# Expert 0's all-token columns cut from 512 to 256, its rows picked by one-hot products, and one weight piece split in halves

## What is computed

```python
def moe_swiglu(h, w_router, w_gate, w_up, w_down):
    t = h.reshape(B * S, Dm)
    logits = (t @ w_router).astype(jnp.float32)
    top_vals, top_idx = lax.top_k(logits, TOP_K)
    top_w = jax.nn.softmax(top_vals, axis=-1)
    gates = jnp.sum(jax.nn.one_hot(top_idx, N_EXPERTS) * top_w[..., None], axis=1)
    for e in range(N_EXPERTS):
        ye = swiglu(t, w_gate[e], w_up[e], w_down[e])
        out = out + gates[:, e:e + 1] * ye
```

## Time and profile before

| | |
|---|---|
| median of three runs | 1045.84 us (1043.88 to 1045.89) |
| the profiled execution | 1044.83 us, of which 1043.1 us from the first to the last instruction (the span) |
| PE busy | 1022.6 us, 98% |
| DVE, ACT, POOL busy | 270.5, 250.6, 54.4 us |
| mean granted clock of PE | 0.995 of full speed |
| weights and other data moved by DMA | 347.24 MB |

### The profile page before, as it was taken

The page is one execution under the profiler, slowest core; times in us unless marked ns, Lnnn a source line. Parts: engine busy times, 40 slices in busy tenths (PEclk is TensorE's granted clock), DMA queues, the critical chain, the costliest instruction groups (busy, mean ns, idle before and its releaser), DMA issues.

```text
span 1043.1 us, 22297 instructions
## 1 busy us (share of the span) xinstructions
PE 1022.6 (98%) x9903; PEld 579.3 (56%) x9903; DVE 270.5 (26%) x418; ACT 250.6 (24%) x426; POOL 54.4 (5%) x159
## 2 busy tenths in 40 slices
PE   8999999999999899999999999999999999999995
PEld 8987888888998654433334444444444444444331
DVE  7677545455677420000000000000000000000022
ACT  7666525345685200000000000000000000000121
POOL 4000000000101000001000001001000100100110
PEclk9999999999999999999999999999999999999998
DMA  8477656552638899999999999999999999999994
GB/s 286 180 253 273 194 179 202 183 178 80 201 113 311 290 357 361 417 419 408 419 409 417 419 418 408 417 420 408 417 418 420 399 419 419 394 393 419 417 417 164
DMA packets 125149, 347.24 MB, mean 333 GB/s; under 512 B 7368, under 2 KB 40176, under 8 KB 125056
## 3 DMA queue, kind: packets, MB, share of 16 engines
q1 hardware_dynamic: 119760, 331.64, 82.0%
q0 software_dynamic: 4560, 13.41, 3.7%
q10 hardware_dynamic: 736, 0.80, 0.2%
HBM read 341.10 MB, written 4.72 MB: 332 GB/s over the span
## 4 chain that ended last, share of the span: by engine, by line
PE 91%; DMA 4%; DVE 2%; issue 1%; ACT 1%; SPq 0%; DVEq 0%; ACTq 0%; POOLq 0%
PE ps L2011 29%; PE ps L2064 14%; PE ps L2015 10%; PE ps L1543 8%; PE ps L1545 8%; PE ps L1544 8%; PE ps L2069 5%; DMA raw_gu<-in_w_in 2%; DMA ring<-in_moe_w_down 2%; PE ps L2026 1%; DMA gains<-tok_rows,tok_row 1%; PE ps L2099 1%; PE ps L1550 0%; PE ps L1932 0%; PE ps L1717 0%
## 5 line engine op out<-in xcount | busy, mean ns | idle before, releaser
L2011 PE MATMUL ps<-ring,xg 128*32 128x512 f32 (+1 forms) x3072 | 379.6, 551 | 0.0
L2064 PE MATMUL ps<-ring,moe_ht 128*32 128x512 f32 x1408 | 177.3, 593 | 1.9 <-DMA ring<-in_moe_w_down 1.9
L2015 PE MATMUL ps<-ring,xg 128*32 128x256 f32 x2048 | 176.4, 379 | 0.0
L2011 PEld LDWEIGHTS ps<-ring,xg 128*32 128x32 f32 x3072 | 111.2, 110 | 95.7 <-issue 50.1
L2015 PEld LDWEIGHTS ps<-ring,xg 128*32 128x32 f32 x2048 | 73.2, 110 | 147.2 <-issue 147.2
L1543 PE MATMUL ps<-hi_gu,xt_hi 128*128 128x512 f32 (+1 forms) x352 | 132.1, 375 | 1.3 <-DVE lo_gu L2203 0.7
L1545 PE MATMUL ps<-hi_gu,xt_lo 128*128 128x512 f32 (+1 forms) x352 | 129.1, 367 | 0.0
L1544 PE MATMUL ps<-lo_gu,xt_hi 128*128 128x512 f32 (+1 forms) x352 | 128.8, 366 | 0.0
L1438 ACT ACTIVATE moe_silu<-ps 128x512 f32<-128x512 f32 (+1 forms) x24 | 13.3, 553 | 334.4 <-PE ps L2015 278.7
L2701 DVE COPY moe_ht<-ps 128x256 f32<-128x256 f32 (+1 forms) x18 | 7.1, 395 | 295.6 <-PE ps L2037 295.6
L2069 PE MATMUL ps<-ring,moe_ht 128*32 128x256 f32 x1056 | 81.1, 379 | 0.0
(11 more groups left out here) (326 smaller groups left out, 880.3 us busy)
## 6 DMA issues: line engine op xcount, KB each, us to landing
ring<-in_moe_w_down SPq DMA_DIRECT2D x88, 1024.0 KB, 16.7
ring<-in_moe_w_gate SPq DMA_DIRECT2D x56, 1024.0 KB, 17.5
ring<-in_moe_w_up SPq DMA_DIRECT2D x56, 1024.0 KB, 17.8
ring<-in_moe_w_gate SPq DMA_DIRECT2D x40, 768.0 KB, 16.4
ring<-in_moe_w_up SPq DMA_DIRECT2D x40, 768.0 KB, 14.3
...
raw_d<-in_dense_w_down SPq DMA_DIRECT2D x11, 1024.0 KB, 4.9
```

Of the source, the lines that this page charges most:

```text
L2011: last = pe.matmul(ps[tile(q), (B_GATE, B_UP)[part], 0:w // 2], xg[:, rows_at, k, tile(g)], weights[:, h * w // 2:(h + 1) * w // 2], start ...
L2015: last = pe.matmul(ps[tile(q), (B_GATE_B, B_UP_B)[part], 0:FC], xg[:, rows_at, k, A_SLOTS:SLOTS], weights[:, q * FC:(q + 1) * FC], start=k ...
L2064: last = pe.matmul(ps[tile(q), B_YA, :], moe_ht[:, at:at + 32], weights[:, h * 512:(h + 1) * 512], start=start, stop=stop)
```

## The change

- The all-token columns of expert 0 become 256 gate and 256 up columns. `FIRST_PIECES` is 2: a first piece now holds four steps k of 512 columns (gate and up side by side, one bank per tile), and `all_piece(j, t)` has 4 x 3 = 12 matmuls of 512 columns.
- Expert 0's remaining 2560 columns are chunks of 1024, 1024 and 512. A 512-column chunk has four k in a piece (two pieces for gate, two for up), and its B slots take 128 columns each in four strips. The first `down` has one piece instead of two; `pick_hidden` has 4 matmuls instead of 8.
- The order on PE is: piece 0 of tile 0, `route(0)`, half of piece 1, `turn_rows` of tile 1, the other half, `route(1)`, piece 0 of tile 1, `find_places`, piece 1 of tile 1, `pick_rows`. VectorE makes the low part of piece 1 in two halves, one before tile 1's post norm and one between it and tile 1's pre norm; ScalarE and VectorE no longer split pieces 2 and 3.
- `pick_rows` makes `xg` of expert 0 by 16 products of `rows` with expert 0's one-hot rows. The DMA gather, its transposes and VectorE's copy of expert 0's token numbers are gone. `xg` lies no longer over `rows` but over `gains[2]` and `pool_w_sb`.
- The ring's slots come in another order: pieces 4 and 5 wait for the splits of the mixing part, 6 to 9 for the output products, 10 and 11 for the splits of the two first pieces, 12 to 15 for `first_used`.

The core of the diff:

```diff
-B_LOGITS, B_PLACES, B_COUNTS, B_ALL, B_XG0 = 4, 4, 7, ((0, 1), (5, 6)), (3, 7)
+B_LOGITS, B_PLACES, B_COUNTS, B_ALL, B_XG0 = 4, 4, 7, (0, 5), (3, 7)
...
-    FIRST_PIECES = 4
+    FIRST_PIECES = 2
...
-    RING_ORDER = [4, 5, 14, 15] + [first_slot(j) for j in range(FIRST_PIECES)] + \
+    EARLY_SLOTS = [first_slot(j) for j in range(FIRST_PIECES, 4)]
+    RING_ORDER = [4, 5, 14, 15] + EARLY_SLOTS + [base + n for n in EARLY_SLOTS for base in (6, 10)] + \
+        [first_slot(j) for j in range(FIRST_PIECES)] + \
         [base + first_slot(j) for j in range(FIRST_PIECES) for base in (6, 10)]
 
     def width(p, c):
 
         if c < 0:
-            return WIDE
-        return 3 * FC if p == 0 or c == CHUNKS - 1 else 4 * FC
+            return FC
+        if c < CHUNKS - 1:
+            return 4 * FC
+        return 3 * FC if p else 2 * FC
 
     def col0(p, c):
 
         if c < 0:
             return 0
-        return WIDE + c * 3 * FC if p == 0 else c * 4 * FC
+        return c * 4 * FC + (0 if p else FC)
+
+    def b_width(p, c):
...
+    def k_tiles(p, c):
+
+        return 2 if width(p, c) > 2 * FC else 4
+
+    def gate_pieces(p, c):
+        return KT // k_tiles(p, c)
...
-                to = flat_piece(raw_gu, slot).rearrange("p (k w c) -> p k w c", k=2, w=2)
+                to = flat_piece(raw_gu, slot).rearrange("p (k w c) -> p k w c", k=4, w=2)
                 for part, w in enumerate((moe_w_gate, moe_w_up)):
-                    sp.dma_start(to[:, :, part, :], w[0, 0][2 * j * P:(2 * j + 2) * P, 0:WIDE]
+                    sp.dma_start(to[:, :, part, :], w[0, 0][4 * j * P:(4 * j + 4) * P, 0:FC]
                                  .rearrange("(k p) n -> p k n", p=P)).then_inc(gu_loaded[slot // 2][slot % 2], 16)
 
             def first_use(n):
@@ -811,10 +826,14 @@
                     sp.wait_ge(d_lo_done, 2 * NCH)
                 elif n < 4:
                     sp.wait_ge(attn_mm, TT * DEPTH)
-                elif n < 8:
-                    sp.wait_ge(gu_lo_done, PIECE0 + n - 4 + 1)
+                elif n < 6:
+                    sp.wait_ge(gu_lo_done, PIECE0)
+                elif n < 10:
+                    sp.wait_ge(out_mm, TT * DEPTH)
+                elif n < 12:
+                    sp.wait_ge(gu_lo_done, PIECE0 + n - 10 + 1)
                 else:
-                    sp.wait_ge(first_used, (n - 8) // 2 + 1)
+                    sp.wait_ge(first_used, (n - 12) // 2 + 1)
...
-                    w, c0 = width(p, c), col0(p, c)
-                    sp.dma_start(ring[:, slot, 0:2 * w].rearrange("p (k n) -> p k n", k=2),
-                                 expert_rows((moe_w_gate, moe_w_up)[part], e)[i * FC:(i + 1) * FC, c0:c0 + w]
+                    w, c0, kn = width(p, c), col0(p, c), k_tiles(p, c)
+                    sp.dma_start(ring[:, slot, 0:kn * w].rearrange("p (k n) -> p k n", k=kn),
+                                 expert_rows((moe_w_gate, moe_w_up)[part], e)[i * kn * P:(i + 1) * kn * P, c0:c0 + w]
                                  .rearrange("(k p) n -> p k n", p=P)).then_inc(ring_loaded[slot], 16)
...
-            gather_picked(0)
-            pool.wait_ge(tok_row_ready, 2)
-            pool.wait_ge(picked_turned, 2)
             gather_picked(1)
...
-                split_first(l, 2)
                 pre_ffn(l, 1)
-                split_first(l, 3)
...
-            def find_rows(n, some):
-                pe.wait_ge(onehots_ready, n + 1)
-                for e in some:
+            def find_rows():
+                pe.wait_ge(onehots_ready, 2)
+                for e in range(1, E):
...
-            def all_piece(j, t, between=None):
+            def all_piece(j, t, steps=(0, 1, 2, 3)):
 
                 hi, lo = flat_piece(hi_gu, first_slot(j)), flat_piece(lo_gu, first_slot(j))
                 a = slice(t * P, (t + 1) * P)
-                for k in range(2):
-                    kt = 2 * j + k
-                    if (j, t, k) == (2, 0, 0):
-                        pe.wait_ge(first_k_lo, 1)
-                    elif t == 0:
+                if t == 0:
+                    if j == 1 and steps[0] == 0:
+                        pe.wait_ge(half_piece_lo, 1)
+                    else:
                         pe.wait_ge(gu_lo_done, PIECE0 + j + 1)
-                    if k and between:
-                        between()
-                    for part in range(2):
-                        at = slice((2 * k + part) * WIDE, (2 * k + part + 1) * WIDE)
-                        last = mm3(ps[:, B_ALL[t][part], :], xt_hi[:, kt, a], xt_lo[:, kt, a], hi[:, at], lo[:, at],
-                                   kt == 0, kt == KT - 1)
+                for k in steps:
+                    kt, at = 4 * j + k, slice(k * WIDE, (k + 1) * WIDE)
+                    last = mm3(ps[:, B_ALL[t], :], xt_hi[:, kt, a], xt_lo[:, kt, a], hi[:, at], lo[:, at], kt == 0, kt == KT - 1)
                 if t == 1:
                     last.then_inc(first_used, 1)
-                elif j == 3:
+                elif j == FIRST_PIECES - 1 and steps[-1] == 3:
                     last.then_inc(all_tile0, 1)
 
             def first_chunk():
                 all_piece(0, 0)
-                all_piece(1, 0)
                 pe.wait_ge(router_lo_done, 1)
                 route(0)
-                all_piece(2, 0)
+                all_piece(1, 0, (0, 1))
                 turn_rows(1, T_FFN, 1)
-                all_piece(3, 0)
+                all_piece(1, 0, (2, 3))
                 xt_ready(1, T_FFN, 1)
                 route(1)
                 all_piece(0, 1)
                 find_places()
-                all_piece(1, 1, lambda: find_rows(0, range(1)))
-                all_piece(2, 1)
-                all_piece(3, 1, turn_first)
-
-            def turn_first():
-                pe.wait_ge(counted, 1)
+                all_piece(1, 1)
                 for part in range(2):
-                    turn_picked(0, part)
+                    pick_rows(part)
+
+            def pick_rows(part):
+                pe.wait_ge(*((counted, 1) if part else (onehots_ready, 1)))
+                for k in range(4):
+                    at = slice((part * 4 + k) * P, (part * 4 + k + 1) * P)
+                    for t in range(TT):
+                        last = pe.matmul(ps[:, B_XG0[part], k * SLOTS:(k + 1) * SLOTS], rows[:, t, at],
+                                         onehots[:, t, 0, 0:SLOTS].bitcast(F32), start=t == 0, stop=t == TT - 1)
+                last.then_inc(picked_turned, 1)
 
...
-                for k in range(4):
+                for k in range(2):
...
-                    pe.wait_ge(*((all_silu, 1) if part == GATE else (all_hidden, 1)))
+                    pe.wait_ge(all_hidden, 1 if part == GATE else TT)
                 else:
                     pe.wait_ge(silu_ready if part == GATE else hidden_ready, n)
+                kn = k_tiles(p, c)
                 for k in range(KT):
-                    slot = piece_ring(p, c, part, k // 2)
-                    if k % 2 == 0:
-                        pe.wait_ge(ring_loaded[slot], piece_level(p, c, part, k // 2, step))
-                    weights = ring[:, slot, (k % 2) * w:(k % 2 + 1) * w]
+                    slot = piece_ring(p, c, part, k // kn)
+                    if k % kn == 0:
+                        pe.wait_ge(ring_loaded[slot], piece_level(p, c, part, k // kn, step))
+                    weights = ring[:, slot, (k % kn) * w:(k % kn + 1) * w]
                     for q in range(4):
                         h, g = divmod(q, 2)
                         last = pe.matmul(ps[tile(q), (B_GATE, B_UP)[part], 0:w // 2], xg[:, rows_at, k, tile(g)],
                                          weights[:, h * w // 2:(h + 1) * w // 2], start=k == 0, stop=k == KT - 1)
                     if has_b(p):
-                        for q in range(w // FC):
-                            last = pe.matmul(ps[tile(q), (B_GATE_B, B_UP_B)[part], 0:FC], xg[:, rows_at, k, A_SLOTS:SLOTS],
-                                             weights[:, q * FC:(q + 1) * FC], start=k == 0, stop=k == KT - 1)
-                    if k % 2:
+                        wb = b_width(p, c)
+                        for q in range(b_groups(p, c)):
+                            last = pe.matmul(ps[tile(q), (B_GATE_B, B_UP_B)[part], 0:wb], xg[:, rows_at, k, A_SLOTS:SLOTS],
+                                             weights[:, q * wb:(q + 1) * wb], start=k == 0, stop=k == KT - 1)
+                    if k % kn == kn - 1:
                         last.then_inc(ring_used, 1)
...
-                split_first(l, 1)
+                split_half_piece(1, 0)
                 post_norm(l, POST_MIX, 1, banks(B_OUT[1], 2))
-                split_first(l, 2)
+                split_half_piece(1, 1)
                 pre_norm(l, PRE_FFN, 1)
-                split_first(l, 3)
                 low_part(l, T_FFN, 1)
...
-                dve.wait_ge(tok_row_mm, 1)
```

(7 more changed lines are left out.)

82 lines of the change are left out of this document (38 added, 44 removed).

## The result

The changed kernel takes **1032.8 us** (median of four runs, 1030.6 to 1033.4) against 1045.9 for the kernel before beside it (1043.9 to 1049.5): ratio 0.987, 95% interval 0.984 to 0.990, so 13 us faster. The forecast was 1034.6, a gain of 11.2. Run twice more beside the experiments, the changed kernel gave 1031.2 and 1031.6, both at a ratio of 0.987. The profiled execution took 1030.6 (span 1028.2, mean granted clock 0.996).

A forecast was written before the change was run, and what follows sets the result against it. It took TensorE's path as the bound, the weight stream close behind. Terms of -9.9, -0.9 and -0.4 sum to -11.2 us, from 1044.83 to 1033.6 profiled, median 1034.6; 80% range 1031.5 to 1038.5.

The forecast's parts named there:

- Part 1: Tile 1's norm chain up to route(1): fewer first-piece products and half splits gain 3.0 us, with 2.6 us new PE idle.
- both covers: Piece 1's half splits on VectorE hide behind ScalarE's root and square; uncovered, each would cost 1.2 us.
- Part 2: From route(1)'s start to expert 0's first gate product: 19.2 us becomes 12.35, a gain of 6.9.
- Part 3: PE's clock, at half from 363.1 to 366.5 us: without long waits, 0.9 us behind the first gate product comes back.
- I take no fall: The new PE waits of 1.6, 1.0 and 0.7 us were taken as too short to halve the clock.
- Part 4: Expert 0's chunks of 1024, 1024 and 512 columns instead of 768: 0.4 us gained in all.
- Part 5: Weight stream: earlier loads of larger pieces move it 12 to 13 us forward, PE 11.2, so PE's gain holds.
- the full ring in p = 6: At expert p = 6 the full ring restores the stream's relation to PE, so the last down-weight waits stay some 2 us.
- Rival (a): The stream was the real bound at the end: the last four waits, 1.9 us, go, giving 1032.7 us; chance 0.12.
- Nothing in this part adds or takes time: On the weight stream: its earlier start and reordered loads were priced at zero in the sum.
- Rival (c): Early loads stay held in SyncE's queue, so p = 1 waits: gain only 4 to 6 us, 1040.8; chance 0.08.
- the 1.7 us around the span: Execution time outside the profiled span, 1044.83 us against 1043.1, kept unchanged in the forecast.

The follow-up runs named there:

- whole: Changed kernel with the low part of first piece 1 split whole ahead of tile 1's last norm, instead of in halves: 1034.8 us, ratio 0.990.
- gather: Changed kernel with the old look-up, copy, indirect load and transposes for expert 0's columns put back instead of the one-hot products: 1039.6 us, ratio 0.995.
- before_pick: Kernel before with only expert 0's columns made by 16 one-hot products instead of the DMA gather: 1041.3 us, ratio 0.996.
- late4: Changed kernel with only ring pieces 8 to 11 held back until tile 1's product of the first piece is done: 1033.8 us (two runs).

## Why the prediction was right, and where not

- **Part 1**: turn_rows(1), named at 339.0, began at 337.67, and route(1), named at 342.5, at 341.12; with the 1.3 us of the start added back, 338.96 and 342.41. Waits 1.43 and 0.97 for 1.6 and 1.0. Gain 3.07 for 3.0; both covers stood as said, and *whole*, with the whole split ahead of the post norm, shows a price of 0.8 us.
- **Part 2**: pick 3.71 for 3.9, copy wait 0.57 for 0.66, distance 12.24 for 12.35. The first gate product, named at 354.8, began at 353.36, or 354.65 with the 1.3 us. Both experiments on it came out near their numbers; only gather's clock fall was three times the length I gave it.
- **Part 3**: "I take no fall" failed as a statement on the kernel: it held in the profiled execution and not in two repetitions, where PE lost 1.6 us. Its bound, 3.4 us at half, is what they show. Whether the short waits bring that fall is **open**: with the waits as they are five of nine profiles show one at 339 to 348 us, with them filled none of two, but over all runs 6 of 13 of the changed kernel and 5 of 10 of the filled ones have a mean granted clock of 0.995 or less. That mean does not tell where a fall was. The six at or under 0.995 average 1033.0 us and the other seven 1031.0.
- **Part 4**: the sign held (0.7 us gained, 0.4 forecast), two terms of it were off and nearly cancel, and one addition was wrong. I took 0.27 us for eight B records of 128 columns; they take 0.22:

```profile
412.64 0.61 PE L2025 MATMUL ps<-ring,xg 128*32 128x256 f32 x8
413.08 0.40 PE L2030 MATMUL ps<-ring,xg 128*32 128x128 f32 x8
413.30 0.61 PE L2025 MATMUL ps<-ring,xg 128*32 128x256 f32 x8
```

  A step of the short chunk is 0.65 to 0.66 us (starts 412.64 and 413.30), and the two short chunks' gate and up are 10.7 us, not 11.2. The nearest row was the wrong guide; streaming (0.21), which I had as the lower end, was right. The four of 1024 columns took 10.45 each from start to the next line's start, not 10.35: 0.4 more. And four times 10.35 and 11.2 are 52.6, not the 52.8 that I wrote; by my own terms the loss was 0.2 there, and measured it is 0.1. By the Trainium skill (TensorE: Matmul & The Clock Gate, section "Wait — 56ns, not 53.3ns?") starts are at least about 25 ns apart; the 27 ns a record here agree with it, lying just above.
- **Part 5 and the end**: the last step of the mechanism failed, and it is the largest miss. The size was right: the stream moved forward by 12 to 13 us, I wrote, and PE by 11.2. The fourth last piece now comes 14.4 us earlier, 13.1 without the start, and PE 11.6. But I went on: "the full ring in p = 6 brings both to the same relation as now", so the waits stay. They did not: 0.9 us instead of 1.9 in this profile, 0.3 and none in the repetitions, whose clock fall kept PE back. By the rows the relation is not made in p = 6. There a piece of the kernel before takes 12.3 us from issue to landing, twice the 6.3 us of gate pieces in 380:395; by that the stream had not caught up with the free slots as it had in p = 0, though its rate dips there too (370 GB/s in 905:930), for a reason that stays open. It is made in p = 0, where the new order of loads holds the stream at the slots until about 440 us instead of 410, and it was kept from there: in 910:920 it is 9.9 us to landing, a shorter queue. For a change of PE's path alone my sentence holds: before_pick and gather moved PE by 4.0 and 8.9 us and the fourth piece by 3.5 and 8.7. Whether the larger pieces of p = 0 or the earlier releases make the difference is not shown by a run of its own; late4, with the larger pieces but late releases, ends like the old order (waits 2.4 us), which points to the releases. Rival (a) gave such a gain 0.12 and priced it at 1.9; it came to 1.5 us at the waits in this profile.
- "Nothing in this part adds or takes time" was too strong. With pieces 4 to 11 held back to 346 us the whole gain is lost (1044.0), with 8 to 11 held back about 2 us of it. Rival (c) named the danger and promised 4 to 6 us of gain even then; with all eight held back none was left, but that run holds them longer than rival (c) does.

Within the spans of the two profiles the change brought 13.6 us (14.9 with the start) for 11.2: 0.1 more in parts 1 and 2, 0.3 in part 4, 2.0 at the end. I had also carried the 1.7 us around the span over unchanged; they became 2.4. So the two profiled executions lie 14.2 us apart, 3.0 more than forecast, 1.3 of it the late start of the one before. The medians lie 13.0 apart, since the changed kernel's is 2.2 above its profiled execution and the other's 1.0: that the forecast median missed by only 1.8 us is in part luck.
